# A mixed decode layer on one Trainium2 core: key pages in five places on a new timetable, stacked query rows, and half of the value pages read earlier

## The reference

```
mod = silu(c) @ w_ada + b_ada                      # six parts: shift, scale, gate, twice
h = rmsnorm(x, g_pre_mix) * (1 + sc1) + sh1
q_sb, k_sb, v_sb, q_g, k_g, v_g, r_g, g_low = split(h @ w_in)
k_past = cache_k[page_table];  v_past = cache_v[page_table]
z = q . k / sqrt(128) + bias
a = exp(log_sigmoid(z) + sum over later keys of log_sigmoid(-z))
o_sb = rmsnorm(a @ v)
S_t = diag(alpha_t) S_{t-1} + k_t^T v_t;  o_t = q_t S_t     # GLA, per head
x = x + gt1 * rmsnorm(concat(o_sb, rmsnorm(o_g) * silu(r_g)) @ w_out)
x = x + gt2 * rmsnorm(swiglu(h2))
```

## Time and profile before

| | us |
|---|---|
| median of 3 runs | 1688.33 |
| the profiled execution | 1688.65 |
| its span, first to last instruction | 1687.1 |
| PE busy | 1532.2 (91%) |
| DVE busy | 937.0 (56%) |
| ACT busy | 644.4 (38%) |
| POOL busy | 137.0 (8%) |
| DMA, mean over the span | 233 GB/s |

### The profile page before, as it was taken

One profiled execution on the slowest core, in us unless ns is written; L12 is line 12 of the kernel. 1 busy time (PEld: TensorE's weight loads), 2 busy tenths in 40 slices (PEclk: granted clock), 3 DMA queues, 4 the chain that ended last, 5 costly groups with the idle time before them and its releaser, 6 DMA issues.

```text
span 1687.1 us, 29455 instructions
## 1 busy us (share of the span) xinstructions
PE 1532.2 (91%) x11490; PEld 1346.7 (80%) x11490; DVE 937.0 (56%) x1014; ACT 644.4 (38%) x1213; POOL 137.0 (8%) x253
## 2 busy tenths in 40 slices
PE   5869967788789999989969999999999999999996
PEld 2237856676677776778739999999999999999995
DVE  1344467887654744433476666666666665445444
ACT  0023345565533434323323433344434433334332
POOL 0001211111234433100000000000000000000000
PEclk7879997898989989989989999999999999999999
DMA  9998988888778886668884556655566665555551
GB/s 344 389 356 291 337 295 278 270 272 260 258 241 293 307 279 208 222 233 302 287 340 137 176 180 181 184 176 178 170 190 182 175 183 178 183 177 183 177 174 52
DMA packets 139315, 392.31 MB, mean 233 GB/s; under 512 B 13906, under 2 KB 18169, under 8 KB 126409
## 3 DMA queue, kind: packets, MB, share of 16 engines
q1 hardware_dynamic: 117746, 317.23, 56.7%
q0 software_dynamic: 21488, 74.00, 12.9%
HBM read 382.14 MB, written 9.04 MB: 232 GB/s over the span
## 4 chain that ended last, share of the span: by engine, by line
PE 70%; DVE 9%; DMA 7%; ACT 6%; issue 5%; POOLq 1%; SPq 1%; POOL 0%; ACTq 0%; DVEq 0%
PE ps L1574 20%; PE ps L1575 19%; PE ps L1576 19%; DVE k_pages L1096 4%; ACT k_pages L694 4%; PE ps L1507 3%; DMA ada_s<-in_w_ada 2%; DMA ada_r<-in_w_ada 2%; ACT w_hi L623 2%; PE ps L1700 1%; DMA v_pages<-in_cache_v 1%; DMA vec_rows<-in_g_gla_out 1%; DVE w_lo L1049 1%; PE ps L1537 1%; POOLq L517 1%
## 5 line engine op out<-in xcount | busy, mean ns | idle before, releaser
L1574 PE MATMUL ps<-h_hi,w_hi 128*128 128x264 f32 x2304 | 678.6, 295 | 35.2 <-ACT proj_t L630 18.1
L1575 PE MATMUL ps<-h_lo,w_hi 128*128 128x264 f32 x2304 | 667.4, 290 | 0.0
L1576 PE MATMUL ps<-h_hi,w_lo 128*128 128x264 f32 x2304 | 666.0, 289 | 0.0
L1574 PEld LDWEIGHTS ps<-h_hi,w_hi 128*128 128x128 f32 x2304 | 447.4, 194 | 81.4 <-issue 60.6
L1448 DVE TENSOR_TENSOR w_lo<-raw,w_hi 128x1024 fp32r<-128x1024 f32 x260 | 314.7, 1214 | 295.3 <-ACT w_hi L892 293.9
L1575 PEld LDWEIGHTS ps<-h_lo,w_hi 128*128 128x128 f32 x2304 | 446.9, 194 | 0.0
L1576 PEld LDWEIGHTS ps<-h_hi,w_lo 128*128 128x128 f32 x2304 | 445.4, 193 | 0.0
L892 ACT ACTIVATE w_hi<-raw 128x1024 fp32r<-128x1024 f32 x264 | 278.1, 1059 | 404.8 <-PE ps L1576 404.8
L1049 DVE TENSOR_TENSOR w_lo<-raw,w_hi 128x1024 fp32r<-128x1024 f32 x132 | 163.0, 1238 | 313.7 <-ACT w_hi L623 313.6
L623 ACT ACTIVATE w_hi<-raw 128x1024 fp32r<-128x1024 f32 x128 | 134.3, 1053 | 244.4 <-PE ps L1576 204.9
L1575 PE MATMUL ps<-act_lo,w_hi 128*128 (+1 forms) x704 | 200.4, 285 | 0.0
(11 more groups left out here) (290 smaller groups left out, 1248.2 us busy)
## 6 DMA issues: line engine op xcount, KB each, us to landing
ada_r<-in_w_ada SPq DMA_DIRECT2D x64, 1024.0 KB, 8.3
raw<-in_w_in SPq DMA_DIRECT2D x96, 512.0 KB, 6.0
raw<-in_w_ffn_gate SPq DMA_DIRECT2D x88, 512.0 KB, 3.7
raw<-in_w_ffn_up SPq DMA_DIRECT2D x88, 512.0 KB, 3.9
raw<-in_w_ffn_down SPq DMA_DIRECT2D x88, 512.0 KB, 3.7
ada_s<-in_w_ada SPq DMA_DIRECT2D x32, 1024.0 KB, 11.0
k_pages<-in_cache_k POOLq DMA_DIRECT2D x64, 512.0 KB, 4.9
v_pages<-in_cache_v POOLq DMA_DIRECT2D x128, 256.0 KB, 4.3
```

Source lines behind the costliest of these rows:

```text
L1574: mm(out, w_hi, xh, start=first, stop=False)
L1575: mm(out, w_hi, xl, start=False, stop=False)
L1576: return mm(out, w_lo, xh, start=False, stop=last)
```

## The change

- Key pages have five places for pages n mod 5 (the fifth moves twice to other free room, with two added waits on POOL), and a new timetable: 18 pages in slots 20 to 31, 18 in 32 to 49, 28 in 50 to 68. Before, there were 11 for every 16 slots, from 20 to 63.
- ACT makes the sums of an odd page one step after DVE's product (`KP_AT.get(st - 1)`).
- The high and the low half of the query rows lie in one matrix of 40 rows, and one product takes the place of two. Some query rows go to other PSUM banks and slots.
- The first two levels of the tree are masked by ACT, which copies blocks (`tree_blocks`), in place of DVE's `tree_mask`.
- The value pages of samples 0 to 3 are loaded in two new places (`v_pairs`) and used in slots 56 to 74, 4 groups in 5 slots. Those of samples 4 to 7 are used in slots 77 to 92. POOL's list is now written as one loop over slots.
- The GLA states of the samples start two slots later (62), the heads of the attention stand at every second slot from 76, the first two blocks of key rows are stored at slots 73 and 74, and the first `dec_select` goes from 86 to 75.
- SP reloads the input rows at s = 102 without a wait for `rows_out`, which moves behind the last weights of token mixing; PE's transposes of them start at slot 109.

The core of the diff:

```diff
-        QHI = put("q_rows_hi", [TS, HS], F32R, at=at_pv)
+        QHL = put("q_rows", [32 + TS, HS], F32R, at=at_pv)
...
-        PG = put("k_pages", [P, 4, HS], at=r0 + 38016)
+        KPG = [put(f"k_page{i}", [P, HS], at=a) for i, a in enumerate(
+            (r0 + 38016, r0 + 42112, r0 + 46208, r0 + 50304, r0 + 62592, r0 + 21120, r0 + 92544))]
         PGV = put("v_pages", [P, 2, 4, 512], at=r0 + 38016)
+        VPA = [[put(f"v_pair{i}{j}", [P, 2, 512], at=a) for j, a in enumerate(two)] for i, two in enumerate(
+            ((r0 + 80000, r0 + 88320), (r0 + 84096, at_pk + 4224)))]
...
-        KP_SLOT = [20 + 11 * n // 16 for n in range(TS * PAGES)]
+        KP_SLOT = [20 + 2 * n // 3 if n < 18 else 32 + n - 18 if n < 36 else 50 + 2 * (n - 36) // 3 for n in range(TS * PAGES)]
         KP_AT = {s: [n for n in range(TS * PAGES) if KP_SLOT[n] == s] for s in KP_SLOT}
-        QB_SLOT = [s + h for s in (17, 22, 28, 33, 39, 44, 50, 55) for h in range(2)]
+        KP_PLACE = [n % 5 if n % 5 < 4 else 4 if n < 34 else 5 if n < 54 else 6 for n in range(TS * PAGES)]
+        QB_SLOT = [s + h for s in (17, 22, 27, 35, 43, 49, 56, 61) for h in range(2)]
+        QB_BANK = [7] * 12 + [4] * 2 + [5] * 2
...
-        DEC_SLOT = [60 + e + (1 if e >= 7 else 0) for e in range(24)]
+        DEC_SLOT = [62 + e + (1 if e >= 11 else 0) for e in range(24)]
...
-        AV_AT = {64 + v: v for v in range(32)}
-        SB_SLOT = [73, 75, 78, 80, 83, 85, 88, 90]
+        AVA_AT = {56 + 5 * p // 4: p for p in range(16)}
+        AVB_AT = {77 + v: v for v in range(16)}
+        SB_SLOT = [76 + 2 * h for h in range(H)]
         SB_AT = {s: h for h, s in enumerate(SB_SLOT)}
+        DROW_AT = {65: 0, 75: 1, 85: 2, 93: 3}
...
-        XT_AT = {106 + k: k for k in range(KC)}
-        STATE_AT = {60 + 3 * c: c for c in range(3, 8)}
-        KT_AT = {85: 0, 87: 1, 90: 2, 93: 3}
+        XT_AT = {109 + k: k for k in range(KC)}
+        STATE_AT = {DEC_SLOT[3 * c - 7] + 6: c for c in range(3, 8)}
+        KT_AT = {73: 0, 74: 1, 87: 2, 88: 3}
...
-                if s == 104:
+                if s == 102:
...
-                    sp.wait_ge(rows_out, 64)
-                    sp.dma_start(XS[:, :], x_sample.rearrange("b o d -> (b o) d")).then_inc(xr_in, 16)
+                    for i in range(2):
+                        sp.wait_ge(ktok_out[i], 32)
+                    sp.dma_start(XS[32:32 + TS, :], x_sample.rearrange("b o d -> (b o) d")).then_inc(xr_in, 16)
...
+            sp.wait_ge(rows_out, 64)
...
-                if n >= 4:
-                    pool.wait_ge(k_odd if n % 2 else k_even, (n - 4) // 2 + 1)
-                elif n == 2:
+                if n == 2:
                     pool.wait_ge(ada_used, 16)
-                pool.dma_start(PG[:, n % 4, :], pool_k[bass.ds(page, 1), :, :].rearrange("o p n -> p (o n)"))\
-                    .then_inc(kpage_in[n % 4], 16)
+                if n == 34:
+
+                    pool.wait_ge(alp_ready, 1)
+                if n >= 5:
+                    pool.wait_ge(k_odd if (n - 5) % 2 else k_even, (n - 5) // 2 + 1)
+                if n == 54:
+
+                    pool.wait_ge(g_o, GH)
+                pool.dma_start(KPG[KP_PLACE[n]][:, :], pool_k[bass.ds(page, 1), :, :].rearrange("o p n -> p (o n)"))\
+                    .then_inc(kpage_in[n % 5], 16)
...
+            def v_pairs(p):
+
+                half, b, grp = p // 8, p % 8 // 2, p % 2
+                if p == 0:
+                    pool.wait_ge(kft_tr, 1)
+                elif p == 1:
+                    pool.wait_ge(g_st, 1)
+                    pool.wait_ge(vg_tr, 4)
+                    pool.wait_ge(vsmp_ready, 1)
+                else:
+                    pool.wait_ge(av_used, p - 1)
+                for j in range(4):
+                    v_load(VPA[p % 2][j // 2][:, j % 2, :], b, 4 * grp + j, half, vpair_in[p % 2])
...
-            for n in range(56):
...
+            for s in range(20, 97):
+                for n in range(5, TS * PAGES):
+                    if s == KP_SLOT[n - 5] + (n - 5) % 2:
+                        k_page(n)
+                if s == 53:
+                    v_pairs(0)
+                if s == 55:
+                    v_pairs(1)
+                if s == 56:
+                    pool.wait_ge(sfin_ready, 1)
+                    pool.dma_start(new_state_prompt[0, 0].rearrange("h k v -> k h v"), SFIN[:, :, :]).then_inc(sfin_out, 16)
+                if s == 58:
+                    key_masks(0)
+                if s in AVA_AT and AVA_AT[s] < 14:
+                    v_pairs(AVA_AT[s] + 2)
+                if s in (70, 71):
+                    v_unit(s - 70)
+                if s in AVB_AT and AVB_AT[s] < 14:
+                    v_unit(AVB_AT[s] + 2)
...
+            def tree_blocks(n):
+
+                act.wait_ge(t_mm, n + 1)
+                half = LEVELS[n]
+                for a in range(0, P, 2 * half):
+                    for tb in range(TB):
+                        ins = s.activation(ATT[a:a + half, 2 * tb, :, a + half:a + 2 * half],
+                                           ps[a:a + half, 5 + tb, :].rearrange("p (h t) -> p h t", h=GH)[:, :, a + half:a + 2 * half],
+                                           ACT.Copy)
+                ins.then_inc(t_mask, 1)
...
+                if st in (34, 36):
+                    tree_blocks((st - 34) // 2)
...
-                for n in KP_AT.get(st, ()):
+                for n in KP_AT.get(st - 1, ()):
...
-                if 34 <= st <= 48 and st % 2 == 0:
+                if 38 <= st <= 48 and st % 2 == 0:
...
-                mm(ps[:, 7, :], pick, QHI[:, cs], start=True, stop=False)
-                mm(ps[:, 7, :], pick, QLO[:, cs], start=False, stop=True).then_inc(qb_mm, 1)
+                mm(ps[:, QB_BANK[i], :], pick, QHL[:, cs], start=True, stop=True).then_inc(qb_mm, 1)```

Where instructions moved, in three places. ACT, steps 20 to 23: `w_hi` is the split of the weights three slots ahead, and its place `raw_in3` is that of step 20; `k_pages` (now `k_page`) with `k_mul` are the sums of an odd page. Before:

```order
L623 ACTIVATE w_hi<-raw 128x1024 [waits unit_used,raw_in3]
L694 ACTIVATE k_pages,z_dec<-k_pages 128x128 [waits k_mul]
L694 ACTIVATE k_pages,z_dec<-k_pages 128x128 x7
L623 ACTIVATE w_hi<-raw 128x1024 [waits unit_used,raw_in0]
L623 ACTIVATE w_hi<-raw 128x1024 [waits unit_used,raw_in1]
L694 ACTIVATE k_pages,z_dec<-k_pages 128x128 [waits k_mul]
```

More of the change, by code:

```diff
@@ L513, in v_unit @@
                 else:
-                    pool.wait_ge(av_used, v - 1)
+                    pool.wait_ge(av_used, 16 + v - 1)
                 for j in range(4):
[L516 to L520, removed]
+                    v_load(PGV[:, v % 2, j, :], b, 4 * grp + j, half, vpage_in[v % 2])
             def key_masks(h):
@@ L594, in _ @@
             act.wait_ge(consts, 1)
-            s.activation(IDR[:, :], ident[0:TS, 0:TS], ACT.Copy).then_inc(idr_ready, 1)
             act.wait_ge(tr_done, 1)
@@ L637, in evac_frees @@
                     act.wait_ge(t_mask, 8)
+                if g == 7:
+                    act.wait_ge(k_even, 25)
+                    act.wait_ge(k_odd, 25)
+                if g == 9:
+                    act.wait_ge(av_used, 16)
                 if g == 8:
@@ L676, in q_rows @@
                 act.wait_ge(srow_tr, 1)
+                act.wait_ge(pick_ready, 2)
                 for half in range(2):
-                    ins = s.activation(QHI[:, half * 512:half * 512 + 512], ps[0:TS, 6 + half, :], ACT.Copy)
+                    ins = s.activation(QHL[0:TS, half * 512:half * 512 + 512], ps[0:TS, 6 + half, :], ACT.Copy)
                 ins.then_inc(srow_ready, 1)
@@ L686, in q_bcast @@
                     act.wait_ge(k_odd, 4 * (b - 1))
[L687 removed]
+                s.activation(QBC[:, b % 2, half * 512:half * 512 + 512], ps[:, QB_BANK[i], :], ACT.Copy).then_inc(qb_ready, 1)
             def page_sums(n):
@@ L720, in dec_rows @@
                 act.wait_ge(av_used, 8 * i + 8)
-                if i >= 2:
-                    act.wait_ge(d_sel, 1)
-                s.activation(DOUT[i % 2][:, :], ps[:, 7, :], ACT.Copy).then_inc(dout_ready, 1)
+                if i == 0:
+                    act.wait_ge(g_o, GH)
+                s.activation(DOUT[i][:, :], ps[:, 7, :], ACT.Copy).then_inc(dout_ready, 1)
             def sb_logs(h):
@@ L755, in k_tok @@
                     act.wait_ge(ktok_out[i % 2], 16)
-                s.activation(KTOK[i % 2][:, :], ps[:, 4, :], ACT.Copy).then_inc(kt_ready, 1)
+                s.activation(KTOK[i % 2][:, :], ps[:, KT_BANK[i], :], ACT.Copy).then_inc(kt_ready, 1)
             def v_tok(i, bank):
@@ L819, in _ @@
                     gla_result(2 * (st - 58) + 1)
-                if st == 59:
+                if st == 61:
                     act.wait_ge(srow_tr, 3)
                     for j in range(2):
-                        ins = s.activation(VGS[:, j * 512:j * 512 + 512], ps[0:TS, 7 if j == 0 else 4, :], ACT.Copy)
```

(37 more changed lines are left out.)

214 lines of the change are left out of this document (108 added, 106 removed).

## The result

The changed kernel takes 1612.99 us (median of 4 runs, 1611.68 to 1616.39) against 1688.87 us for the kernel before in the same rounds: a ratio of 0.9553, interval 0.9536 to 0.9571. A later comparison gave 1613.02 and 0.9541 (0.9518 to 0.9563). The forecast was 1665, with 1638 as the lower end of its range: the sign was right, the gain of 76 us is three times the 23.5 forecast. The profiled execution took 1614.1 us, 74.5 less than that of before.

A forecast was written before the change was run, and what follows sets the result against it. ACT and DVE waiting for each other were taken to leave PE idle in slots 20 to 65. Terms -7.5 - 17.5 + 0 + 10.5 - 5 - 4 = -23.5 from 1688.65 gave 1665 us, range 1638 to 1688.

The forecast's parts named there:

- The loop: Slots 20 to 65: ACT waits 105.5 us for DVE's key page product, DVE 73.2 us for ACT's split of weights.
- The signs set for it: Slots 20 to 63: ACT's wait for DVE's product falls from 105.5 us to under 30, DVE's from 73.2 to under 40.
- A: Slots 20 to 31: late sums take ACT's wait away, DMA time of 67 us remains of 74.8; term -7.5 us.
- B: Slots 32 to 49: key pages go from 26 to 18, PE's work and waits leave 95 of 112.6 us; term -17.5.
- D: Slots 56 to 65: more key pages and value groups, DMA sets 75 us against 64.3; term +10.5 us.
- all of it comes out: Rival, whole kernel: little idle time left, PE also stays at its upper clock level; -55, 1634 us; chance 0.20.
- C: Slots 50 to 55: a value group is added, DMA takes 40 us against 39.4, some idle time goes; term 0.
- E and F: Slots 66 to 95, set by PE: six value groups fewer, two state products more, less idle time; term -5 us.
- G: Slots 96 to 108: SP's wait for stores and PE's 3.0 us wait for a modulation row go; term -4 us.
- the ring of four: Key page places before the change: no long DVE wait for a key page load, so not the limit; no size given.
- Lockstep of the value groups: Rival, slots 56 to 65: POOL stands at each group for PE, 107 us for 64.3, total 1698 us; chance 0.12.
- Present pace: Rival, slots 20 to 95: loads keep their pace, slots 20 to 49 already ran at DMA speed; total 1689 us; chance 0.13.

The follow-up runs named there:

- e7: The changed kernel with the first two levels of the tree masked by DVE again in place of ACT's block copies: 1615.94 us, ratio 0.9561.

## Why the prediction was right in the mechanism and wrong in the size

**The loop.** Right. Late sums alone give 52 us, undoing them costs 50, and the two waits of the earlier trace rows are down to 11.4 and 34.3 us. The signs set for it (under 30, under 40) came. Those set for the stages did not: A is 50.0 us and not 63 to 70, B 82.4 and not 88 to 102; D came at over 290 GB/s, but 63.5 us is not longer than 64.3 (the later profile has 65.0).

**The step that failed** is the pace of a stage whose DMA is the limit: "315 GB/s for a stage whose DMA is the limit: between 305, which slots 66 to 75 hold at share 0.90, and 336". The rows of before were taken as a ceiling, and the "all of it comes out" rival was marked down because A "would need 364 GB/s, more than any stage here has held". In A of before 282 GB/s came from loads that were asked for late, not from engines at their limit: with the loop gone and nothing else changed, the same stage holds 366. The runs hold 378 in A and 389 in D. The trace of before had it too, outside the stages of the earlier trace rows: 411 GB/s at share 1.00 from 60 to 90 us, and behind token mixing, in both with loads of 512 KB and 1 MB from SP's queue alone, in packets mostly of 8 KB:

```profile
837.20:882.10 44.90, 28.43 (x164) 13.65 (x162) 34.80 (x66) 13.54 (x18) 0.00 (x0) 0.86 0.92 378
```

Term by term:
- A: -24.8 for -7.5. Forecast 21.1 / 0.315 = 67; measured 18.9 MB / 0.378 = 50.0. The rate is 11 us of the miss; the other 6 are 2.2 MB fewer, nearly all of weights and modulation rows (12 and 5 loads issued in the stage before, 11 and 4 now). The "work is the same" of the prediction held for the key pages alone.
- B: -30.2 for -17.5. DVE's 17.7 us were about right (its busy time falls by 15.8 against before, by 18.1 against the late sums alone), but the stage was put on PE at the clock of before, 91 us, plus 4 of waits. With the waits gone PE stays at its upper level: 81.97 us busy in 82.4. The forecast named that 82 and did not take it; e7's masks show DVE standing just behind.
- C: -7.0 for 0. 12.6 MB at 315 were 40 us; 10.6 MB came, at 326. But DMA is no limit here: with half columns C takes the same 32.4 us at 263 GB/s. What is left is PE's 29.4 us of work (33.5 before, at a granted clock of 0.87 for 0.95 now) and 3.0 of a wait for the tree; late sums alone bring the stage to 30.3. So the loop held C too, and a DMA time was put under a stage that DMA doesn't end.
- D: -0.8 for +10.5. The 5 value groups and 7 key pages did come, with 1.1 MB of state loads out of C (24.7 MB for 14.3), at 389 GB/s for 315. Against the late sums alone, where D takes 56.1 us, they do cost 7.4, so the sign of the step was right.
- E and F: -7.1 for -5. E gained nothing (+1.2). F fell by 8.3 (132.6 to 124.3): PE has 6.1 us less of work there, more than the four value groups that left at 1.0 each, at a granted clock of 0.99 for 0.95.
- G: -4.1 for -4, and 6 by the run that undoes it. SP's stop and PE's 3.0 us went as said.

The misses, -17.3, -12.7, -7.0, -11.3 and -2.1, are the 50 us between forecast and profile. Half of it is the DMA rate (11 us in A, 14 in D, where 23.7 MB at 389 would have been 61 us), a quarter PE's clock and waits in B, the rest the DMA limit that C doesn't have and bytes that moved between stages.

From 358 GB/s as the most for one core the prediction worked out that D could not be under 66 us; D took 63.5, and 65.0 in the later profile. The Trainium skill ("HBM Reference", Specifications (TRN2)) calls 358 the share when both cores of a pair stream, and says that a core alone goes well above it, to about 425. The measured 378 to 389 agree with that.

**The fifth place** was taken as nothing by itself ("the ring of four is not what holds it"). True of before and nearly so of A to C; in the new kernel it is worth 14.7 us by the medians, and of the 20.2 us in the profile of the run without it 15 are in D and E.

**The rivals.** Lockstep of the value groups: refuted, PE waits 6.9 us in all for them from slot 56 to 75 and D is 63.5 us, not 107. Present pace: refuted by A. "All of it comes out" was the right one, and still some 20 us too slow, by A (8 us), C (7), B and D (5 each), while E to G gave 6 less than it has.

## What to carry to other kernels

A GB/s at a share below 1, measured while requests arrive late, is no ceiling: dividing it by the share misjudges it too. Before a DMA limit is put under a stage, look through the whole trace for a stretch where loads queue up behind one another, as there was here before slot 20 and behind token mixing; where there is none, keep both ends, and give the case in which every wait falls together its full chance. A wait that closes a loop over two engines hides clock, places and transfers behind it, and their worth can only be read after it is gone.

## What the runs showed of the hardware

- The time that a DMA engine spends on a packet is not fixed by its size: from share and packets in A (16 x 74.8 x 0.84 / 6747, 16 x 50.0 x 0.99 / 5970), a packet of much the same mean size (3.1 and 3.2 KB) takes 149 ns in the kernel before and 133 in the changed one. The mix of sizes is not the reason: counted in the traces packet by packet, those of 4096 B take 197 and 170 ns in the mean, those of 2048 B 104 and 91, those of 8192 B 334 and 318. The medians hardly differ (159 and 160, 84 and 84, 309 and 314): before, some packets took much longer than the rest. At its medians the 21.1 MB of A in the kernel before would take 52 us, 405 GB/s, an estimate that its trace allowed. Why the slow ones are slow, no run here settles.
- The share can read 1.00 at 279 GB/s (half the rows of a page, into partitions 0 to 63) and 0.99 at 378 (all rows). Half the columns, as many bytes as half the rows, read 0.95 at 346, so it goes by which partitions are loaded. A full share is no measure of bytes.
- Kernels that load the same up to slot 20 reach it between 197.2 and 204.1 us in their profiles, the changed kernel itself at 200.9 and 197.2; that alone moves whole times by some us, so stage lengths compare better than totals.
